# Last stage of a hybrid encoder step: cross scores behind level 2, level 3 moved into the group of levels 4 to 7

## The reference, cut to what matters

```
A     = cumsum(log_f)                                  # decay, per head and channel
attn  = einsum('bthk,btshk,bshk->bhts', q, exp(A_t - A_s) (s <= t), k)
o     = attn @ i + (q * exp(A)) @ S
S_new = exp(A_last) * S + (k * exp(A_last - A)).T @ i
o     = rmsnorm(o) per head
cross = softmax(xq @ mem_k / 8) @ mem_v                # 4 heads of 64
y     = concat(o, cross) * silu(gate);   x = x + y @ w_out;   final rmsnorm
```

## Time and profile before

| | us |
|---|---|
| median of 3 runs | 2423.72 |
| lowest and highest | 2419.04, 2426.49 |
| the profiled execution | 2424.32 |
| its span in the trace | 2422.6 |
| PE busy | 2332.1 (96%) |
| DVE busy | 1822.3 (75%) |
| ACT busy | 1421.2 (59%) |
| POOL busy | 382.5 (16%) |

### The profile page before, as it was taken

The page is one execution under the profiler, slowest core; times in us unless marked ns, Lnnn a source line. Parts: engine busy times, 40 slices in busy tenths (PEclk is TensorE's granted clock), DMA queues, the critical chain, the costliest instruction groups (busy, mean ns, idle before and its releaser), DMA issues. The chain is left out here.

```text
span 2422.6 us, 61529 instructions
## 1 busy us (share of the span) xinstructions
PE 2332.1 (96%) x23677; PEld 2084.9 (86%) x23677; DVE 1822.3 (75%) x3555; ACT 1421.2 (59%) x3281; POOL 382.5 (16%) x585
## 2 busy tenths in 40 slices
PE   7999999999999999999998999999999989999998
PEld 5999999999867777777777898999999978888886
DVE  7888787877666555555555899798888778888885
ACT  4554666755565545454544565676757566666664
POOL 2332000000022111111111332000000021212111
PEclk9999999999999999999999999999999989999999
DMA  6887887879883222222224888787779693443442
GB/s 234 297 292 236 288 282 219 250 238 318 244 263 100 85 82 64 81 65 81 71 79 147 275 292 273 233 277 228 247 236 322 224 304 94 135 142 119 130 138 69
DMA packets 396663, 469.62 MB, mean 194 GB/s; under 512 B 39860, under 2 KB 248556, under 8 KB 396376
## 3 DMA queue, kind: packets, MB, share of 16 engines
q1 hardware_dynamic: 379832, 406.02, 53.5%
q0 software_dynamic: 14704, 54.92, 6.6%
q10 hardware_dynamic: 1840, 4.75, 0.8%
HBM read 318.77 MB, written 151.56 MB: 194 GB/s over the span
## 5 line engine op out<-in xcount | busy, mean ns | idle before, releaser
L1460 PE MATMUL pj_acc<-x_lo,pj_wh 128*128 128x256 f32 (+1 forms) x3080 | 780.4, 284 | 0.0
L1460 PE MATMUL pj_acc<-x_hi,pj_wh 128*128 128x256 f32 (+1 forms) x3080 | 780.3, 284 | 0.0
L1460 PEld LDWEIGHTS pj_acc<-x_lo,pj_wh 128*128 128x128 f32 x3080 | 578.2, 188 | 0.0
L1460 PEld LDWEIGHTS pj_acc<-x_hi,pj_wh 128*128 128x128 f32 x3080 | 578.2, 188 | 0.0
L503 ACT ACTIVATE pj_wh<-pj_wt 128x512 fp32r<-128x512 f32 x676 | 420.7, 634 | 263.0 <-DMA pj_wt<-tsum 169.4
L510 DVE SCALAR_TENSOR_TENSOR pj_wl<-pj_wt,pj_wh 128x512 fp32r<-128x512 f32 x676 | 469.2, 712 | 89.5 <-ACT pj_wh L503 81.7
L1456 PE MATMUL pj_acc<-x_hi,pj_wl 128*128 128x256 f32 (+1 forms) x3080 | 509.6, 287 | 15.6 <-DVE pj_wl L510 13.5
L1456 PEld LDWEIGHTS pj_acc<-x_hi,pj_wl 128*128 128x128 f32 x3080 | 425.0, 188 | 24.5 <-DVE pj_wl L510 21.7
L1301 DVE TENSOR_TENSOR pj_out<-pj_out,pj_acc 128x512 f32<-128x512 f32 (+1 forms) x448 | 321.4, 718 | 101.6 <-PE pj_acc L1460 69.9
L2643 ACT ACTIVATE pb_se<-pb_se,pb_mn 128x640 f32<-128x640 f32 (+4 forms) x208 | 156.1, 751 | 106.5 <-DVE pb_mn L2493 106.2
L2493 DVE CUSTOM_DVE_ANT_0 pb_se<-pb_SC,pb_bias 128x640 f32<-128x640 f32 (+4 forms) x204 | 144.5, 726 | 52.7 <-PE pb_SC L2295 47.9
(11 more groups left out here) (364 smaller groups left out, 4103.1 us busy)
## 6 DMA issues: line engine op xcount, KB each, us to landing
pj_wt<-tsum SPq DMA_DIRECT2D x546, 256.0 KB, 3.9
proj<-pj_out SPq DMA_DIRECT2D x112, 512.0 KB, 4.2
tsum<-pj_wt SPq DMA_DIRECT2D x140, 256.0 KB, 3.1
pj_wraw<-in_w_in_dram POOLq DMA_DIRECT2D x24, 1024.0 KB, 6.6
tsum<-pj_wraw SPq DMA_DIRECT2D x56, 256.0 KB, 4.4
hg_x<-x_mid SPq DMA_DIRECT2D x17, 512.0 KB, 3.5
pb_gate<-proj SPq DMA_DIRECT2D x16, 512.0 KB, 4.9
pb_x<-in_x_prompt_dram SPq DMA_DIRECT2D x16, 512.0 KB, 3.5
```

The costliest lines, as they stand in the source:

```text
L1460: ins = nc.tensor.matmul(BANK[j][:, 0:n], w.hi[j][:, k], x.of(y, p, j)[:, k], start=False, stop=(k == 3 and i == 1))
```

## The change

Three places change. In `order_of` level 3 takes its bank after the state update, no longer before it. On PE `cross_scores(t)` runs directly behind level 2 and so ahead of `turn_outputs(t, 0)`, and level 3 runs as the first of the group 3 to 7 behind `cross_values`. On DVE `place(t, 3)` stands behind `add(t, 0)`, directly ahead of places 4 and 5.

```diff
-            return [0, 1, 2, ("x", 0), ("x", 1), 3] + kv + [4, 5, 6, 7]
+            return [0, 1, 2, ("x", 0), ("x", 1)] + kv + [3, 4, 5, 6, 7]
...
                     level(t, 2)
+                    cross_scores(t)
                     if t:
                         turn_outputs(t, 0)
                         project(t - 1, LATE + 2, LATE + 4)
                         turn_outputs(t, 1)
                         project(t - 1, LATE + 4, CHUNKS)
-                    cross_scores(t)
-                    level(t, 3)
                     project(t, 0, 3)
...
                     cross_values(t)
-                    for i in (4, 5, 6, 7):
+                    for i in (3, 4, 5, 6, 7):
                         level(t, i)
...
                     least(t, 0)
                     least(t, 1)
-                    place(t, 3)
                     step(t, 3)
...
                     add(t, 0)
+                    place(t, 3)
                     place(t, 4)
                     place(t, 5)
                     step(t, 7)
```

## The result

The changed kernel takes 2465.49 us (median of 5 runs, 2461.37 to 2471.45), the kernel before 2423.72 beside it: a ratio of 1.0174, 95% interval 1.0149 to 1.0200. It is slower, as forecast, but by 41.8 us where 11 were forecast, and outside the range.

The account below looks back on a forecast made before the run. PE was taken as the bound, nearly gapless, with DVE late for place 1. A loop of 12.72 + 13.78 = 26.50 us, 14 times 371.0 (+9.8), with small terms +11, gave 2434.7 us; range 2423 to 2444.

Parts of the forecast that it names:

- The new wait at C: On PE behind level 2, the cross scores wait for place 1 on DVE: a stall of 1.27 us.
- C: The start of the cross scores on PE in a tile, forecast at T + 12.72 us.
- T: The start of level 4 on PE in a tile; the next one was forecast at C + 13.78 us.
- From C to the gate: From cross scores on PE to gate(t, 0) on DVE: 0.73 + 0.33 + 0.58 = 1.64 us.
- PE by itself is there at ... C + 6.94: When PE, without waiting, would reach update(t-1, 1): 6.94 us after the cross scores start.
- The second wait, at update(t-1, 1): On PE ahead of the second update half, waiting for exp(t, 0) until C + 7.59: 0.65 us.
- The rival with only the first wait: exp(t, 0) comes 0.65 us earlier against PE, so the loop is 25.85 us and the total 2425; chance 0.16.
- Place 3: On DVE ahead of places 4 and 5: the same 0.26 us in its new position, costed at nothing.
- Odd gaps: Irregular gaps of PE's loads, longest 2.33 us: most swallowed by the new stall, up to 1.7 us to be added.
- the rival's +35 us: The clock falls after the new gaps, half of 5 us in each of 14 tiles: +35, total 2470; chance 0.04.
- a sign of being wrong: The clock leaving 1.00, scores within 0.4 us of level 2's end, or a loop under 26.0 or over 27.0 us.
- Changes of shape: PE's drain between tiling modes: 0.33 us taken behind the cross scores, one change fewer left in a tile.

Follow-up runs that it names:

- e3: The changed kernel with update(t-1, 0) moved ahead of project(t, 0) on PE: 1.0121 of the kernel before.
- e2: The kernel before with only level 3, its bank and its place moved as in the change, cross scores left behind project(t-1, 15): 1.0061 of the kernel before.
- e5: The changed kernel with turn_outputs(t, 0) ahead of cross_scores(t) on PE: 1.0146 of the kernel before.
- e9: The changed kernel with cross scores behind both turn_outputs but ahead of project(t-1, 15): 1.0110 of the kernel before.
- e1: The kernel before with only the cross scores moved directly behind level 2: 1.0102 of the kernel before.
- e7: The kernel before with level 4 moved between cross_turn and project(t, 6): 1.0007 of the kernel before.
- e8: The kernel before with both update halves one project step later and level 4 between cross_turn and project(t, 6): 1.0006 of the kernel before.

## Why the prediction was wrong

- **The new wait at C: right.** C = T + 12.72 was forecast. Level 4 starts a third of the run of levels 3 to 5 behind 2150.47, at about 2150.95; C is 2163.66, 12.71 later. The stall is 1.27 as forecast.
- **From C to the gate: right.** 1.68 us against 1.64 (2163.66 to 2165.34), with the 0.33 for the change of shape.
- **The step that failed: "PE by itself is there at ... C + 6.94".** The sum took PE from the end of project(t-1, 15) straight into project(t, 0). But project(t, 0) writes the bank that add(t-1, 1) must have read, and the code has a wait for it. In the kernel before, that add ended in the shadow of the scores and level 3, at 2144.12 (the row below), with PE arriving at 2144.28; the change takes both away and sets the add back by the gate's delay. I had followed DVE past the add, to the minima and exp, and never asked who on PE waits for it. It measured 1.49 us a tile, 20.8 in 14 loops; e3 (filling it with work shortens the loop) and e2, e5 and e9 (its length follows what stands ahead of the add) show it.

```profile
2143.44 0.68 DVE L3176 TENSOR_TENSOR hg_x<-hg_x,hg_OP 128x512 f32<-128x512 f32 x1
```

- **The second wait, at update(t-1, 1): did not occur.** The same omission: with 1.49 us more ahead of it, PE comes at C + 8.46 (2172.12), behind exp's C + 7.59. The 0.65 counted there is to be taken off, so the undisturbed loop is 26.50 - 0.65 + 1.49 = 27.34; measured 27.35. The reading of exp itself was right: it ends 5.83 us behind the gate, at 2171.17. The rival with only the first wait had the right outcome for a reason that didn't happen, an earlier exp.
- **Place 3: right, it costs nothing.** From update 1 to the next group (2172.12 to 2177.80) it is 5.68 us against 5.69, and T to C is as forecast.
- **Odd gaps: mis-sized.** "Most odd gaps lie between T and C, where the new stall swallows them" holds in part: the idle ahead of the scores falls to 0.12 to 0.47 in seven tiles, 10.8 us in all where 14 x 1.27 would be 17.8. But I took the gaps as given, where the long run enlarges them beyond what the stall can hide: 12.3 us more instead of some 5 less.
- **What each is worth.** For 14 loops 371.0 us were forecast and 398.4 measured, 27.4 more. The undisturbed loop, 27.35 for 26.50, makes 11.9 of it: the wait for the add that was left out, less the second wait that didn't occur. The other 15.5 are what odd gaps add, with the 1.7 of the clock's dip. Either alone would have put the time past the upper end of the range, 2444.
- **The clock: the rival's +35 us didn't come.** The clock is 1.00 in a loop with idle stretches of 1.27, 0.33 and 1.48 us; the Trainium skill's rule on short idle gaps ("TensorE: Matmul & The Clock Gate", A second HAM failure mode) isn't borne out by these. It did leave 1.00 once, which the prediction named as a sign of being wrong: in tile 13, where odd gaps of 1.67 and 2.00 us came on top of the wait of 1.49. e3 and e5 show one such dip in their loops and e9 two, the others none, e2 with gaps up to 2.39 us among them; the size of a gap alone doesn't decide it, and what does stays open.
- **Changes of shape.** What the Trainium skill says on drains in "TensorEngine Tiling (Array Packing)", Key Properties, agrees with the 0.33 us that the scores' new neighbour shows; the changes of shape come to the same sum, 14.7 and 14.6, since the 0.36 us that fell away stood ahead of the scores, where the stall now is.
- **Who carries how much.** e1 has +1.02%, e2 +0.61%, both together 1.74%: within the intervals the two halves of the change add up, the first by waits, the second by odd gaps.

## What to carry to other kernels

When a step on an in-order engine is moved ahead, go through everything that it now stands in front of, and for each follow the other engine to the next wait back on the first: here the price was not the stall itself but an accumulator bank freed one add later. A step that seems only to occupy PE (level 3) may be what covers such a wait. And many tiny instructions in a row are a cost of their own: look at what the run costs before making it longer. Shortening it further than in the kernel before (e7, e8) brought nothing that could be measured here.

## What the runs showed of the hardware

In this stage PE's loads show gaps with no wait behind them, of 0.7 to 2.4 us, at places in its instruction list that are multiples of some 125 weight loads (250 recorded PE instructions) apart, and only within or just behind a run of small products. Each of the 111 on this spacing ends 1.0 to 1.9 us behind the landing of a 16 KB instruction read. Their sum in the same 14 tiles was 4.1 and 4.3 us where the group was 96 loads long (e7, e8), 4.4 to 11.5 at 144 (6.7 in the kernel before) and 17.1 to 22.7 at 192 (19.0 in the changed one). With 48 loads put in ahead of them, the gaps that had a counterpart stood 47 or 48 loads earlier against the work.
